# Norm statistics gathered on GpSimd beside the output projections, normed tiles handed over in pairs into blocks multiplied by halves

## The reference, cut to what matters

```python
# layers 0 and 1 (both streams, x and xc)
h  = rms_norm(x,  norm_w[layer]) * (1.0 + scale)   + shift
hc = rms_norm(xc, norm_w[layer]) * (1.0 + scale_c) + shift_c
proj = h @ w_in[layer]                      # and hc @ w_in[layer]
...
y = concat([...]) @ w_out[layer]
x = x + gate * y
# the four mixers: h is x itself; the mixer's last step is "@ w_out"
x = layer_norm(ALPHA * x + mixer(x), g, b)  # mean and variance over the 2048 features
```

## Time and profile before

| what | us |
|---|---|
| median of 3 runs (lowest to highest) | 3857.78 (3857.01 to 3860.29) |
| the profiled execution's own time | 3860.46 |
| its span, first to last instruction | 3858.7 |
| TensorE busy | 3472.3 (90%) |
| VectorE busy | 1955.2 (51%) |
| ScalarE busy | 1737.6 (45%) |
| GpSimd busy | 334.4 (9%) |
| mean granted TensorE clock, 1 is full speed | 0.953 |

### The profile page before, as it was taken

How to read it: one execution, slowest core, us unless ns; L and a number is a source line. 1 busy time by engine, 2 the same in 40 slices (tenths; PEclk the granted TensorE clock), 3 DMA queues, 4 the chain that set the end, 5 groups by cost and what they waited for, 6 DMA issues and landing times.

```text
span 3858.7 us, 60131 instructions
## 1 busy us (share of the span) xinstructions
PE 3472.3 (90%) x25857; PEld 3120.7 (81%) x25857; DVE 1955.2 (51%) x2592; ACT 1737.6 (45%) x2573; POOL 334.4 (9%) x521
## 2 busy tenths in 40 slices
PE   7699999999699999999944997999979999799897
PEld 2477767778488999999943997999979989688797
DVE  1432312232355454456678444555546554699754
ACT  1343433221456634455533334555545553566543
POOL 0000001100000000000000000000000000588300
PEclk9899999999899999999967998999999999899899
DMA  9454545522133554555521453554534435233353
GB/s 386 166 173 148 174 164 195 192 104 98 38 121 131 164 180 165 185 181 185 182 104 65 157 182 121 170 168 167 170 126 160 137 130 177 91 124 124 108 180 121
DMA packets 157555, 589.75 MB, mean 153 GB/s; under 512 B 18304, under 2 KB 18384, under 8 KB 155504
## 3 DMA queue, kind: packets, MB, share of 16 engines
q1 hardware_dynamic: 134784, 497.64, 38.0%
q0 software_dynamic: 20704, 73.56, 5.6%
...
...
## 4 chain that ended last, share of the span: by engine, by line
PE 78%; DVE 12%; DMA 4%; ACT 4%; issue 2%; DVEq 0%; POOL 0%; ACTq 0%; SPq 0%; POOLq 0%
PE psum_all L455 22%; PE psum_all L457 22%; PE psum_all L459 22%; DMA raw<-in_stream 2%; DVE w_lo L414 2%; DMA mod_early<-in_stream 2%; PE psum_all L674 2%; PE psum_all L789 1%; DVE s_vd L2549 1%; ACT xT L804 1%; PE psum_all L1053 1%; PE psum_all L1023 1%; PE psum_all L784 1%; DVE ssd_seg L1655 1%; DVE s_re_n L2557 1%
## 5 line engine op out<-in xcount | busy, mean ns | idle before, releaser
L455 PE MATMUL psum_all<-act_hi,w_hi 128*128 128x256 f32 (+1 forms) x6704 | 2043.5, 305 | 142.7 <-DVEq L389 52.4
L457 PE MATMUL psum_all<-act_lo,w_hi 128*128 128x256 f32 (+1 forms) x6704 | 2016.3, 301 | 0.0
L459 PE MATMUL psum_all<-act_hi,w_lo 128*128 128x256 f32 (+1 forms) x6704 | 2015.0, 301 | 0.0
L414 DVE TENSOR_TENSOR w_lo<-raw,w_hi 128x1024 fp32r<-128x1024 f32 x866 | 1071.0, 1242 | 1304.5 <-ACT w_hi L407 1303.6
L455 PEld LDWEIGHTS psum_all<-act_hi,w_hi 128*128 128x128 f32 x6704 | 1291.8, 193 | 233.5 <-issue 142.5
L407 ACT ACTIVATE w_hi<-raw 128x1024 fp32r<-128x1024 f32 x866 | 911.8, 1057 | 968.8 <-DMA raw<-in_stream 943.2
L457 PEld LDWEIGHTS psum_all<-act_lo,w_hi 128*128 128x128 f32 x6704 | 1292.2, 193 | 41.8 <-issue 3.2
L459 PEld LDWEIGHTS psum_all<-act_hi,w_lo 128*128 128x128 f32 x6704 | 1291.0, 193 | 41.9
L648 POOL DMA_DIRECT2D mod_late<-in_stream x128 | 67.8, 534 | 583.2 <-PE psum_all L674 553.9
L1576 POOL COPY ssd_b<-ssd_xbc 128x256 f32 x8 | 3.2, 404 | 1303.9 <-DVEq L1689 1203.1
L1481 DVE SCALAR_TENSOR_TENSOR conv_acc<-conv_x,params,conv_acc 128x255 f32<-128x255 f32 x144 | 69.6, 483 | 56.6 <-ACT conv_x L1475 53.1
...
## 6 DMA issues: line engine op xcount, KB each, us to landing
raw<-in_stream SPq DMA_DIRECT2D x866, 512.0 KB, 3.3
mod_late<-in_stream POOLq DMA_DIRECT2D x128, 512.0 KB, 5.0
mod_early<-in_stream SPq DMA_DIRECT2D x64, 512.0 KB, 8.9
...
```

What stands on the lines that cost most here:

```text
L414: dve.tensor_tensor(w_lo[:, n % RING, :], raw[:, n % RING, :], w_hi[:, n % RING, :].bitcast(F32), ALU.subtract).then_inc(lo_ready, 1)
L455: pe.matmul(sums, w_hi[:, n % RING, cols], block.rhs(kk, True, block.width), start=(kk == 0), stop=False)
L457: pe.matmul(sums, w_hi[:, n % RING, cols], block.rhs(kk, False, block.width), start=False, stop=False)
L459: last = pe.matmul(sums, w_lo[:, n % RING, cols], block.rhs(kk, True, block.width), start=False, stop=(kk == block.kt - 1))
```

## The change

The stages at the seams go. Each flow gets two partners: `behind`, whose statistics run in the slots of the output projections, and `before`, whose finish (`begin_tensor`, `begin_scalar`, `begin_vector`) runs at the start of the next flow, in the same stage.

- **LayerNorm** (four): GpSimd adds the blocks of `xT` as they are taken; after 8 blocks TensorE sums them once, and twice that half sum (the mean, estimated) is subtracted by VectorE (`centre`) and squared by ScalarE (`square`) in slots 10 to 15; GpSimd adds the squares. At the start of the next flow: last block centred and squared, five matmuls instead of 32, variance corrected by the square of (mean - estimate), root, reciprocal.
- **SecondInput** (layer 1): squares of both streams in the output slots, added by GpSimd (128x512); then two matmuls, one root and two reciprocals for both streams.
- **FirstInput** (layer 0) and **Tokens** (SSD): no statistic; the split is done in the flow. `clear_late` (two PSUM banks) moves from the `modulated` stage to the end of the stage before it.
- **Hand-over**: tiles go in pairs (128x512) through scale, gain and bias, high, low; TensorE waits for each pair (`wait_tile`) instead of for a barrier. Two of the four ring units are split between pairs (`split`).
- **Halves**: the first `LEAD` (2 or 3) blocks of those flows are multiplied as k-tiles 0 to 7 of each, then 8 to 15 of each. The weight stream is ordered to match; all later side work stands `LEAD` slots later.
- The last LayerNorm sends its output in four DMAs of 4 tiles, each as its tiles are whole.

The diff, cut to its core:

```diff
+LEAD = dict(gate_in0=2, gate_in1=2, fox_in=3, mla_in=3, s5_in=2)
...
+def by_halves(units, n):
+
+    return [pair[i] for i in range(2) for pair in units[:n]] + [u for pair in units[n:] for u in pair]
+
...
+def halves_first(blocks, n):
+
+    return [Half(block) for block in blocks[:n]] + blocks
...
+        def flow(blocks, banks=4, late=0, tensor_side=None, scalar_early=None, vector_side=None,
+                 gpsimd_side=None, before=None, behind=None, out_at=0):
...
+            def multiply(pe, block, tiles, g):
...
+                for kk in tiles:
+                    n, t = tile_at(block, kk)
+                    if t == 0 or kk == tiles[0]:
+                        pe.wait_ge(lo_ready, n + 1)
+                    if block.wait:
+                        block.wait(pe, kk)
...
-                                    late_tensor(pe, n - n0)
+                if before:
+                    before.begin_tensor(pe)
+                for g, item in enumerate(blocks):
+                    if isinstance(item, Half):
+                        multiply(pe, item.block, range(UNIT_TILES), g)
+                    elif item:
+                        multiply(pe, item, range(UNIT_TILES if item.halved else 0, item.kt), g)
                     if tensor_side:
...
+                if before:
+                    before.begin_scalar(act, lambda i: split_hi(act, n0 + min(2 + (i + 1) // 3, RING)))
                 for g in range(slots):
-                    split_hi(act, last_unit(g) + 1 + AHEAD)
+                    split_hi(act, ends[g] + 1 + AHEAD)
                     if scalar_early:
...
+                    if behind:
+                        behind.scalar(act, g - out_at)
...
+                    if behind:
+                        behind.vector(dve, g - out_at)
...
+                for r in range(KT + 1) if behind else ():
+                    behind.gpsimd(pool, r)
...
+            def make_high(self, act, i):
+                self.wait_whole(act, i)
+                act.activation(self.pairs[i][2], self.pairs[i][0], ACT.Copy).then_inc(self.high.sem, 1)
+
+            def make_low(self, dve, i):
+                src, _, hi, lo = self.pairs[i]
+                self.wait_whole(dve, i)
+                dve.wait_ge(self.high.sem, self.high.at(i + 1))
+                dve.tensor_tensor(lo, src, hi.bitcast(F32), ALU.subtract).then_inc(self.low.sem, 1)
+
+            def make_parts(self, act, ready, split, out=True):
+
+                n = len(self.pairs)
+                for i in range(n):
+                    ready(act, i)
+                    self.whole_scalar(act, i)
+                    if i and out:
+                        self.make_high(act, i - 1)
+                    split(i)
...
+        class LayerNorm(Affine):
...
+
...
+            def sum(self, pe, half):
+
+                pe.wait_ge(self.added.sem, self.added.at((7, 13)[half]))
+                one = pe.matmul(self.sums[half], const("over_d"), self.acc[half][:, :], start=True, stop=not half)
+                if half:
+                    pe.wait_ge(taken["dve"], self.counts[KT - 1])
+                    one = pe.matmul(self.sums[1], const("over_d"), xT[:, KT - 1, :], start=False, stop=True)
+                one.then_inc((self.means if half else self.half_summed).sem, 1)
+
+            def tensor(self, pe, r):
+                if r == 9:
+                    self.sum(pe, 0)
...
+                        .then_inc(self.added.sem, 1)
+                d = self.d
+                steps = {12: [(d[:, 0:4, :], d[:, 4:8, :], 8)], 13: [(d[:, 0:4, :], d[:, 8:12, :], 12)],
+                         14: [(d[:, 0, :], d[:, 12, :], 13)], 15: [(d[:, 1, :], d[:, 13, :], 14)],
+                         16: [(d[:, 0:2, :], d[:, 2:4, :], 14), (d[:, 0, :], d[:, 14, :], 15)]}
+                for n, (to, of, squares) in enumerate(steps.get(r, ()), r - 12):
+                    pool.wait_ge(self.squared.sem, self.squared.at(squares))
+                    if n:
+                        pool.wait_ge(self.squares_added.sem, self.squares_added.at(n))
+                    pool.tensor_tensor(to, to, of, ALU.add).then_inc(self.squares_added.sem, 1)
...
+            def square(self, act, a, end):
+                act.wait_ge(self.centred.sem, self.centred.at(end))
+                act.activation(self.d[:, a:end, :], self.d[:, a:end, :], ACT.Square).then_inc(self.squared.sem, end - a)
+
+            def scalar(self, act, r):
+                if r == 10:
+                    act.wait_ge(self.half_summed.sem, self.half_summed.at(1))
+                    act.activation(self.half[:, :], self.sums[0], ACT.Copy, scale=2.0).then_inc(self.half_ready.sem, 1)
+                if r - 1 in self.at:
+                    self.square(act, *self.at[r - 1])
+                if r == 15:
+                    self.square(act, *self.at[15])
+
...
+            def centre(self, dve, a, end):
+                dve.wait_ge(self.half_ready.sem, self.half_ready.at(1))
+                dve.wait_ge(taken["dve"], self.counts[end - 1])
+                dve.tensor_tensor(self.d[:, a:end, :], xT[:, a:end, :],
+                                  self.half[:, :].unsqueeze(1).broadcast_to([P, end - a, T]), ALU.subtract) \
+                   .then_inc(self.centred.sem, end - a)
...
+            def vector(self, dve, r):
+                if r in self.at:
+                    self.centre(dve, *self.at[r])
...
+            def begin_tensor(self, pe):
+                self.sum(pe, 1)
+                pe.wait_ge(self.squares_added.sem, self.squares_added.at(6))
...
+                for k in (0, 1, KT - 1):
+                    one = pe.matmul(self.var, const("over_d"), self.d[:, k, :], start=(k == 0), stop=(k == KT - 1))
+                one.then_inc(self.vars.sem, 1)
...
+            def begin_vector(self, dve, split):
+                ordered = order["vector"]
+                self.centre(dve, KT - 1, KT)
+
+                dve.wait_ge(self.means.sem, self.means.at(1))
+                dve.scalar_tensor_tensor(out=self.mean[:, :], in0=self.half[:, :], scalar=0.5, in1=self.sums[1],
+                                         op0=ALU.mult, op1=ALU.add).then_inc(ordered.sem, 1)
...
+                dve.wait_ge(ordered.sem, ordered.step())
+                dve.wait_ge(self.vars.sem, self.vars.at(1))
+                dve.tensor_tensor(norm_root[:, :], self.var, self.off[:, :], ALU.subtract).then_inc(self.spread.sem, 1)
+                self.shift(dve, 0)
+                dve.wait_ge(self.rooted.sem, self.rooted.at(1))
+                dve.reciprocal(norm_root[:, :], norm_root[:, :]).then_inc(ordered.sem, 1)
+                dve.wait_ge(ordered.sem, ordered.step())
+                pieces = KT // 2
+                for p in range(pieces + 1):
+                    if p + 1 < pieces:
+                        self.shift(dve, p + 1)
+                    if p < pieces:
+                        self.scale(dve, p)
+                    if p >= 2 and self.out:
+                        self.make_low(dve, p - 2)
+                    split(p)
+                if self.out:
+                    self.make_low(dve, pieces - 1)
+
+            def wait_tile(self, pe, k):
+                pe.wait_ge(self.low.sem, self.low.at(k // 2 + 1))
...
+        class FirstInput(Affine):
...
+            def begin_vector(self, dve, split):
+                for k in range(KT + 1):
+                    if k < KT:
+                        self.whole_vector(dve, k)
+                    if k:
+                        self.make_low(dve, k - 1)
+                    split(k // 2)
...
+        class SecondInput(Affine):
...
+            def gpsimd(self, pool, r):
+                b = r - 1
+                if b in range(1, KT - 1):
+                    pool.wait_ge(self.squared.sem, self.squared.at(b + 1))
+                    if b > 1:
+                        pool.wait_ge(self.added.sem, self.added.at(b - 1))
+                    pool.tensor_tensor(self.acc[:, :, :], self.acc[:, :, :] if b > 1 else self.sq[0][:, :, :],
+                                       self.sq[b % 2][:, :, :], ALU.add).then_inc(self.added.sem, 1)
...
+            def begin_vector(self, dve, split):
...
+                for c in range(5):
+                    for v, (x, y) in enumerate(((xT, self.tmp), (ctxT, ctxT)) if c < 4 else ()):
+                        dve.tensor_tensor(y[:, 4 * c:4 * c + 4, :], x[:, 4 * c:4 * c + 4, :],
+                                          self.root[:, v, :].unsqueeze(1).broadcast_to([P, 4, T]), ALU.mult) \
+                           .then_inc(self.scaled.sem, 1)
+                    if c < 4:
+                        dve.wait_ge(self.scaled.sem, self.scaled.at(2 * c + 2))
+                        for i in range(4 * c, 4 * c + 4):
+                            self.whole_vector(dve, i)
+                    for i in range(4 * c - 4, 4 * c) if c else ():
+                        self.make_low(dve, i)
+                        split(i // 2)
...
```

(8 more changed lines are left out.)

579 lines of the change are left out of this document (334 added, 245 removed).

## The result

| what | before, us | after, us |
|---|---|---|
| median (lowest to highest) of 4 runs each | 3858.56 (3857.01 to 3860.29) | 3741.19 (3736.52 to 3745.46) |
| the profiled execution's own time | 3860.46 | 3739.53 |
| its span | 3858.7 | 3737.7 |
| TensorE / VectorE / ScalarE / GpSimd busy | 3472.3 / 1955.2 / 1737.6 / 334.4 | 3424.8 / 2003.9 / 1738.9 / 444.0 |
| mean granted clock | 0.953 | 0.957 |

The ratio is 0.9695 (95% interval 0.9679 to 0.9712): faster, 117 us by the medians, 3734 forecast. Measured again later, the same kernel took 3737.88, ratio 0.9677 (0.9661 to 0.9692).

The account below looks back on a forecast made before the run. TensorE bounds the kernel (VectorE in S5's input), idling 235.6 us at seams. Savings 20 + 37 + 8 + 15 + 15 + 13.5 + 15.5 - 0.5 = 123.5 from 3860.5 give 3737, less 2.7 to the median 3734; range 3710 to 3764.

Parts of the forecast that it names:

- The end: Last LayerNorm and output after the last matmul: barrier as before, output in smaller DMAs; 15.5 us saved, bounds 13 and 17.
- LayerNorm: Seams after SSD and FoX: TensorE idles 20.2 us against 35.0; 15 us saved each, bounds 10 and 20.
- one of my signs of a wrong forecast: At the seams: clock under 0.8 for more than the first half block would show the forecast wrong.
- Layer 1: Seam at layer 1's two-stream input: idle 19.2 us against 56.0; 37 us saved, bounds 31 and 41.
- Layer 0: Seam at layer 0's input: idle 10.2 us against 29.8; 20 us saved, bounds 17 and 23.
- SSD: Seam before SSD: gap only the barrier, 1.0 us, clock need not fall; 8 us saved, bounds 6.5 and 9.5.
- S5: Seam before S5, VectorE the bound: first state multiply comes sooner; 13.5 us saved, bounds 8 and 17.
- (c): Output slots: GpSimd's adds hold VectorE through the shared port and so w_lo; 92 us lost, 3826; chance 0.03.
- (d): Output slots: VectorE becomes the bound, slower than before; about 4250 if every instruction were stretched 3.7 times; chance 0.02.
- (e): Seams: early first pair gains TensorE nothing, it waits until the last pair; 65.7 us saved, 3792; chance 0.05.
- (b): Seams: slower hand-over, clock stays 1.2 GHz in dense half blocks, ScalarE late for unit 4; 95.5 saved, 3762; chance 0.20.
- (a): Seams: quicker hand-over, high parts hide behind VectorE's passes, splits don't hold it; 147.5 us saved, 3710; chance 0.12.

Follow-up runs that it names:

- the improved kernel: Changed kernel with additions on VectorE, no end barrier, weight splits out of the first four pairs, block 14 centred before the last slot's split: 3714.28 us, 0.9623.

## Why the prediction came out right, point by point

**Number.** 7.2 us too low. 2.6 of it is the saving in the profiled execution, 120.9 against 123.5. Another 4.4 is the step to the median: I took off the 2.7 by which the profiled execution before lay above its median, and the one after lies 1.7 below. The rest is rounding. Executions of the changed kernel spread over 9 to 13 us, those of the kernel before over 3 at first and 12 later; a shift of 2.7 was not worth a term. That the saving comes out so near is in part luck: the end was missed by 6.9 us, and layer 1 gave 5 more than its term.

**The step that failed** is "The end. Last take to barrier as before (no weights left, so centring is early)". Late centring was not the danger. The barrier came 6.0 us behind the last matmul in place of 0.7, because it waits for GpSimd's drain. That is 5.3 us of the 6.9 missed; the rest is in the statistics, as at the seams below. Without the barrier, or with the drain paid early, the span's end is 19.7 to 20.0 us behind the last matmul's end, and 20 was forecast. The rows of the kernel before had the drain's price, 7.08 us in S5; I read only drains that somebody waited for.

**LayerNorm.** 14.0 and 16.0 saved, 15 forecast, but two errors cancel. Start: the barrier 3.0 us behind the last matmul, forecast 2.3, since GpSimd's additions run in a row of 3.7 us; the reciprocal done 6.7 to 7.5 us behind the barrier, forecast 5.5, since the statistics matmuls run at half clock (one, two records, steps at 0.85 us, 0.45 before) and VectorE waits 1.64 and 1.29 us for them. How much this is depends on the execution. The variance's matmuls and VectorE's wait for them, behind SSD in the changed kernel (clock 0.50) and behind FoX in its second profiled execution (clock 1.00):

```profile
2252.71 2.77 PE L999 MATMUL psum_all<-ln_d,consts 128*128 128x256 f32 x6
2255.58 0.42 DVE L1035 TENSOR_TENSOR norm_root<-psum_all,ln_off 128x256 f32<-128x256 f32 x1 [1.29 <-PE psum_all L999]
```

```profile
2780.15 1.53 PE L999 MATMUL psum_all<-ln_d,consts 128*128 128x256 f32 x6
2781.79 0.42 DVE L1035 TENSOR_TENSOR norm_root<-psum_all,ln_off 128x256 f32<-128x256 f32 x1 [0.20 <-PE psum_all L999]
```

In six profiled executions with the same statistics, 18 seams, the reciprocal was done 5.5 us behind the barrier at three, where the clock had not fallen, 7.5 at nine, where it had fallen ahead of the statistics and stayed low, and 6.4 to 6.7 at the other six, where it fell or came back in between. So the forecast's 5.5 was right at the clock it took for granted.

The first pair comes 15.2 to 15.9 us behind the last matmul, not 12.8, and the fourth at 23.5 to 24.2, not 21.7; from the first to the fourth it is 8.3, 9 forecast, and the last `act_lo` is at s+29 to s+30, 28.5 forecast. Against it: the 2.9 us of lower clock that I kept as a loss behind the restart now lies in the wait. The windows above show 0.50 and 0.54 until 2275 and 1.00 from then on, with TensorE busy throughout. (Behind SSD the clock was still low 1 us behind the end of the first half block, so one of my signs of a wrong forecast was met, and it cost next to nothing.) And behind SSD and FoX the second half of block 0 did not wait for the last pair (0.24 us for the seventh behind FoX is all); before S5, with a lead of 2, it waited 1.7 us for pairs. The splits hold the pairs by 2.9 and 3.3 us, 1.69 and 2.02 of waiting and 1.23 each, where I had 2.3 each and 3 for the first. The way to the first pair names three shifts and three scales less one, but counts six passes; the trace has six.

**Layer 1.** First matmul 15.1 us behind the last one, about 15 forecast; last `act_lo` at s+30.8, 32.3 forecast. 42.0 saved, not 37: behind the restart TensorE waits 1.4 us in all, where I had it wait 4 for the last pair. To the layer's first q/k statistic it is 39.2, to its last 41.0; the last 3 us came in the layer, where the code is the same.

**Layer 0.** First matmul 6.9 behind, 7 forecast. Saved to the first q/k statistic 21.2, to the layer's end 17.5. In twelve profiled executions with the same layer 0 its last matmul started at 950.0 to 957.0 us, in this one at 957.0: the 3.7 us are within that, and by their median, 954.5, the saving is 20, as forecast.

**SSD.** 1.6 us in place of 1.0, the clock at 1.00 behind it, 8.5 saved.

**S5.** First state multiply 59.3 us behind the seam before, 46.8 after: 12.5, forecast 13.5.

**Rivals.** (c) and (d) fall: GpSimd's additions do stretch VectorE, up to 1.96 from 1.22 in the mean, and no output slot waits for it; with GpSimd out of it the stretches between seams are the same. (e) falls: TensorE runs from the fourth pair on. (b) is half true, the restart is 3 us later and the clock is low, but in time in which TensorE had nothing to do. (a) is in part what the improved kernel does, by taking the splits out of VectorE's way: 3714, near its 3710. But that kernel also has what (a) had not, the last barrier gone and the additions on VectorE; the additions alone gave 9.5 to 13 us.
